# The softmax of two attentions, taken by pairs of heads instead of head by head

## The chip, the cores and the metric

The kernel runs as one program on one core of a Trainium2 chip. Its time is the device time of one execution in microseconds (us); the runs of a kernel are compared by their median. Five engines work beside each other, each with its own list of instructions in fixed order: TensorE (PE; its weight loads are PEld), VectorE (DVE), ScalarE (ACT), GpSimd (POOL) and SyncE (SP, which only issues transfers here). An engine waits where its list has a wait on a semaphore that another engine counts up.

## The reference

Two blocks of a network work on 256 tokens of width 1024, all in fp32. The first has a recurrent layer and then an attention with 16 heads over a window of 128 tokens; the second has a gated feed-forward network, a mixer of two attentions with 8 heads each, and a second feed-forward network. Two of the three attentions have a softmax. The first has a sink, a learned number per head that takes part in the maximum and the sum but has no value:

```python
    s = jnp.where(valid[None, :, None, None], s + alibi[None, None], -jnp.inf)
    sink = sinks.astype(jnp.float32).reshape(N_KV_HEADS, GROUP)[None, None, :, :, None, None]
    m = jnp.maximum(jnp.max(s, axis=-1, keepdims=True), sink)
    p = jnp.exp(s - m)
    denom = jnp.sum(p, axis=-1, keepdims=True) + jnp.exp(sink - m)
    p = (p / denom).astype(v.dtype)
    o = jnp.einsum('bnkgqs,bnskd->bnqkgd', p, vb)
```

The second (MoBA, 8 heads) is, at this length, a causal softmax attention over all 256 tokens without sinks. Everything else is matrix products with weights that are read once from memory (134 MB).

## The kernel before

Most of the kernel is products with weights. A weight matrix comes in halves of a chunk (128x1024 numbers). SP loads a half into `stage`, ACT rounds it to `w_hi` (helper `hi`, L933), DVE subtracts to get the rest `w_lo` (helper `lo`, L1373), and PE multiplies hi by hi, hi by lo and lo by hi (L480, L488). `w_hi` and `w_lo` are rings of four halves: half n can be made once PE is done with half n-4.

The two softmax attentions stand in the middle of such products. Each is a software pipeline over rounds r, one head to a round, and every engine has its own loop over r. The 128 queries of each of the two token blocks lie on the partitions; a head's scores are 128x384 numbers, block 0 with 128 keys and block 1 with 256, so each head has two maxima, two sums and two exponentials.

- PE, even r: `scores_of_two` (L719) makes the scores of heads r and r+1 in banks 0 and 1; it first waits until both maxima of the two heads before have been taken, since these still read the same two banks. Then, each r from LAG = 4 on, `turn(r-4)` (L731) transposes the normalised probabilities of head r-4 into bank 2 or 3; `turn(n)` waits for head n's normalisation, and for the copy that empties its bank from head n-2 (`t_out` at least n-1). In odd r, from 7 on, `values_of_two` (L738, L741) multiplies with v. At the rounds in `SWA_FILL` a half of a product (24 matmuls) is put in between, in the second attention one half in each round. From r = 17 on the first attention's output product begins (`gated_out`).
- DVE, each r: `masked_max(r)` (L1677) adds the bias or mask, writes the scores to one of five buffers in SBUF, and takes the maxima; the negated maxima `ntop` (L1680) release ACT. `inverse_sum(r-2)` adds the sink's exponential (L1689) and inverts (L1692). Then come the other pieces of `SWA_LO`: a `w_lo`, or copies out of banks.
- ACT, each r: `softmax_exp(r)` takes two exponentials with the negated maximum as bias and the sum as second output, and in the first attention a third, of the sink. Then `turned(r-4)` copies head r-4's transposed probabilities out of bank 2 or 3; only then follows the `w_hi` of `SWA_HI`, if any. After round 15 ACT loads the table for silu, which the gates of the output product need.
- POOL, each r: makes the distance bias of head r+3 (L460) and normalises head r-2 in two instructions (L448, L450).

Heads of the first attention are 0 to 15 below, those of the second are 16 to 23.

## Time and profile before

| | us |
|---|---|
| median of 3 runs (838.83 to 838.92) | 838.84 |
| the profiled execution, whole | 838.82 |
| its span in the trace | 837.0 |
| PE busy / DVE busy / ACT busy / POOL busy | 806.7 / 551.7 / 468.7 / 124.9 |
| first attention, 189 to 230 us: PE busy of 41.0 | 35.22 |
| second attention, 485 to 522 us: PE busy of 37.0 | 37.00 |

Busy times are sums over an engine's instructions, overlaps counted once. The 1.8 us between span and whole are start and end of the program, which no engine's instructions fill. PE is busy for 96% of the span, so only its idle time (30.3 us in all), and what would make it longer, can move the end. In a timeline row the bracket gives the engine's idle time before the instruction and who ended it.

### The profile page before, as it was taken

What the parts mean: (1) busy time and instruction counts of PE and PEld (TensorE: products, weight loads), DVE (VectorE), ACT (ScalarE), POOL (GpSimd) and SP (SyncE); (2) the same over time, 40 slices, a digit from 0 to 9 for tenths busy, and PEclk for the clock granted to TensorE, in tenths of its full rate; (3) what the DMA queues carried; (4) which work ended last, traced back from release to release, by engine and by line L of the source; (5) the groups of instructions that cost most, each with busy time, mean ns of one, the idle gap of its engine ahead of it and who ended that gap; (6) DMA issues with size and microseconds to landing.
All of it is one profiled execution on the core that took longest, in us unless ns stands there. A gap on an engine that the chain in (4) does not pass through costs nothing.

```text
span 837.0 us, 16462 instructions
## 1 busy us (share of the span) xinstructions
PE 806.7 (96%) x6371; PEld 775.1 (93%) x6371; DVE 551.7 (66%) x811; ACT 468.7 (56%) x732; POOL 124.9 (15%) x143
## 2 busy tenths in 40 slices
PE   5999799999899999999999999999999999999997
PEld 5999799897699999999999999998999999999885
DVE  6987995867658766666448755455577766666443
ACT  5679844767856544454345455655747454444433
POOL 9315620215503000000003003000001200000000
PEclk9999899999999999999999999999999999999999
DMA  8624347462236666655655544443545666665651
GB/s 257 211 76 130 122 152 228 128 192 89 95 95 208 202 184 189 180 177 181 193 176 154 179 147 143 134 126 122 179 134 183 192 200 189 186 176 179 181 193 50
DMA packets 104104, 136.35 MB, mean 163 GB/s; under 512 B 5049, under 2 KB 92529, under 8 KB 104049
## 3 DMA queue, kind: packets, MB, share of 16 engines
q1 hardware_dynamic: 102288, 133.26, 51.9%
q0 software_dynamic: 1600, 2.28, 1.0%
q8 instruction: 39, 0.64, 0.3%
q14 instruction: 17, 0.13, 0.1%
q10 hardware_dynamic: 160, 0.05, 0.0%
HBM read 134.51 MB, written 1.05 MB: 162 GB/s over the span
## 4 chain that ended last, share of the span: by engine, by line
PE 74%; ACT 4%; DVE 4%; POOL 3%; issue 1%; POOLq 0%; ACTq 0%; DVEq 0%
PE bank L480 54%; PE bank L540 7%; PE bank L488 7%; POOL arena L432 2%; ACT a_hi L933 2%; DVE w_lo L1373 1%; PE bank L719 1%; ACT w_hi L933 1%; ACT arena L933 1%; PE bank L738 1%; PE bank L731 1%; PE bank L896 1%; DVE arena L1677 1%; PE bank L884 1%; DVE a_lo L1408 0%
## 5 line engine op out<-in xcount | busy, mean ns | idle before, releaser
L480 PE MATMUL bank<-a_hi,w_hi 128*128 128x256 f32 (+1 forms) x1672 | 477.8, 286 | 11.1 <-DVE w_lo L1373 6.2
L480 PE MATMUL bank<-a_lo,w_hi 128*128 128x256 f32 (+1 forms) x1672 | 473.9, 283 | 0.0
L480 PE MATMUL bank<-a_hi,w_lo 128*128 128x256 f32 (+1 forms) x1672 | 473.7, 283 | 0.0
L1373 DVE TENSOR_TENSOR w_lo<-stage,w_hi 128x1024 fp32r<-128x1024 f32 x250 | 317.8, 1280 | 223.0 <-ACT w_hi L933 222.8
L933 ACT ACTIVATE w_hi<-stage 128x1024 fp32r<-128x1024 f32 x250 | 260.6, 1052 | 160.6 <-PE bank L480 115.0
L480 PEld LDWEIGHTS bank<-a_hi,w_hi 128*128 128x128 f32 x1672 | 321.5, 192 | 15.5 <-issue 7.9
L480 PEld LDWEIGHTS bank<-a_lo,w_hi 128*128 128x128 f32 x1672 | 321.7, 192 | 0.0
L480 PEld LDWEIGHTS bank<-a_hi,w_lo 128*128 128x128 f32 x1672 | 321.6, 192 | 0.0
L933 ACT ACTIVATE arena<-arena 128x512 f32<-128x512 f32 (+4 forms) x63 | 37.8, 605 | 76.1 <-DVE arena L1440 42.9
L432 POOL TENSOR_TENSOR arena<-arena 128x512 f32<-128x512 f32 x12 | 23.0, 1925 | 375.1 <-ACT arena L933 374.8
L488 PE MATMUL bank<-w_hi,a_hi 128*128 128x256 f32 x208 | 60.5, 291 | 1.7 <-DVE a_lo L1408 1.7
L488 PE MATMUL bank<-w_hi,a_lo 128*128 128x256 f32 x208 | 58.8, 283 | 0.0
L488 PE MATMUL bank<-w_lo,a_hi 128*128 128x256 f32 x208 | 58.8, 283 | 0.0
L933 ACT ACTIVATE a_hi<-arena 128x512 fp32r<-128x512 f32 (+3 forms) x49 | 29.6, 605 | 50.7 <-DVE arena L1784 15.0
L488 PEld LDWEIGHTS bank<-w_hi,a_hi 128*128 128x128 f32 x208 | 39.8, 191 | 2.9 <-DVE a_lo L1408 1.2
L488 PEld LDWEIGHTS bank<-w_hi,a_lo 128*128 128x128 f32 x208 | 39.9, 192 | 0.0
L488 PEld LDWEIGHTS bank<-w_lo,a_hi 128*128 128x128 f32 x208 | 39.8, 192 | 0.0
L540 PE MATMUL bank<-w_hi,a_lo 128*128 128x512 f32 x88 | 34.3, 390 | 0.0
L540 PE MATMUL bank<-w_hi,a_hi 128*128 128x512 f32 x88 | 34.2, 389 | 0.0
L540 PE MATMUL bank<-w_lo,a_hi 128*128 128x512 f32 x88 | 34.2, 389 | 0.0
L933 ACT ACTIVATE arena<-bank 128x384 f32<-128x384 f32 (+1 forms) x35 | 17.9, 513 | 26.9 <-PE bank L854 7.9
L933 ACT ACTIVATE arena<-arena,ntop 128x128 f32<-128x128 f32 (+1 forms) x48 | 21.4, 446 | 19.9 <-DVE ntop L1680 19.7
(178 smaller groups left out, 670.2 us busy)
## 6 DMA issues: line engine op xcount, KB each, us to landing
stage<-ffn_w_gate SPq DMA_DIRECT2D x44, 512.0 KB, 3.8
stage<-ffn_w_up SPq DMA_DIRECT2D x44, 512.0 KB, 3.8
stage<-ffn_w_down SPq DMA_DIRECT2D x44, 512.0 KB, 3.6
stage<-w_in SPq DMA_DIRECT2D x40, 512.0 KB, 3.5
stage<-a_w_in SPq DMA_DIRECT2D x24, 512.0 KB, 4.8
stage<-b_w_in SPq DMA_DIRECT2D x16, 512.0 KB, 4.0
stage<-a_w_out SPq DMA_DIRECT2D x12, 512.0 KB, 3.8
stage<-b_w_out SPq DMA_DIRECT2D x8, 512.0 KB, 3.6
```

What stands on the lines that cost most here:

```text
L432: pool.tensor_tensor(tiles(SQ + a, w), tiles(SQ + a, w), tiles(SQ + b, w), ALU.add).then_inc(sq_add, 1)
L480: mm = pe.matmul(dst, w[:, slot, c:c + P], a[:, k, :] if isinstance(k, int) else wide(a[:, bass.ds(k, 1), :]), start=start and n == 0, sto ...
L488: mm = pe.matmul(dst, a[:, k, tb * P:(tb + 1) * P], w[:, slot, c:c + n], start=start and i == 0, stop=stop and i == 2, skip_group_check=True)
L540: mm = pe.matmul(token_bank(tb, h)[:, :], a[:, k, t], w[:, slot, c], start=False, stop=w is w_hi and a is a_hi, skip_group_check=True)
L719: mm = pe.matmul(bank[i][:, c:c + w], q[r, t * T + c:t * T + c + P], k[r, 0:keys], start=True, stop=True)
L731: mm = pe.transpose(bank[2 + n % 2][:, c * P:(c + 1) * P], p[:, c * P:(c + 1) * P], ident)
L738: pe.matmul(bank[o][i * HD:(i + 1) * HD, c:c + T], v[i][0], w[i][:, 0:T], start=True, stop=False, skip_group_check=True)
L884: pe.matmul(z[:, 0:T], k[s, 0:P], q[s, 0:T], start=True, stop=True)
L896: pe.matmul(sums[:, 0:SC], con[:, TRI:TRI + P], sp_n, start=True, stop=False, skip_group_check=True)
L933: return nc.scalar.activation(out_, in_, func, **kw)
L1373: dve.tensor_tensor(w_lo[:, n % RING, 0:w], src, w_hi[:, n % RING, 0:w].bitcast(F32), ALU.subtract)\
L1677: dve.tensor_tensor_reduce(s[:, c:c + w], ps[:, c:c + w], bias[:, T - w:T], 1.0, floor, ALU.add, ALU.max, accum_out=top[:, 2 * n + q:2 * n ...
```

## The change

Both softmaxes are done by pairs of heads. On DVE, in even rounds only, `masked_max` runs for heads r and r+1 one behind the other, one instruction then negates all four maxima (`negated`), for the first attention another forms sink minus maximum for both heads, and `inverse_sums` adds and inverts for both heads of the pair before. On ACT, `softmax_of_two` takes the four exponentials of the pair in even rounds, and one of 128x4 for the two sinks, on an input that needs no bias; `turned(r-4)` stays one to a round behind it. POOL's normalisations wait for the pair's inverse. The score buffers go from five to six. PE's list of instructions and its waits are unchanged. The diff:

```diff
--- before.py
+++ after.py
@@ -86,6 +86,7 @@
 SWA_HI = {1: 11, 2: 12, 4: 13, 6: 14, 11: 15, 12: 16}
 SWA_LO = {2: 11, 3: 12, 7: 13, 10: 14, 12: 15, 15: 16}
 LAG = 4
+SCORE_BUFS = 6
 MIX_TURN = {5: 0, 6: 1, 7: 2, 8: 3}
 
 MOBA_FILL = [1] * 12
...
@@ -251,11 +252,11 @@
 
         def score_buf(n):
 
-            return flat[:, 24 * T + n % (LAG + 1) * SC:24 * T + (n % (LAG + 1) + 1) * SC]
+            return flat[:, 24 * T + n % SCORE_BUFS * SC:24 * T + (n % SCORE_BUFS + 1) * SC]
 
         def prob_t(n):
 
-            at = 24 * T + (LAG + 1 + n % 3) * SC
+            at = 24 * T + (SCORE_BUFS + n % 3) * SC
             return flat[:, at:at + SC]
 
         def dist_bias(n):
@@ -443,7 +444,7 @@
             square_sums(1)
             def normalise(n):
 
-                pool.wait_ge(den_inv, n + 1)
+                pool.wait_ge(den_inv, n // 2 + 1)
                 s = score_buf(n)
                 pool.tensor_scalar(s[:, 0:P], s[:, 0:P], rden[:, 2 * n:2 * n + 1], 1.0, ALU.mult, ALU.mult)\
                     .then_inc(p_norm, 1)
@@ -1147,15 +1148,17 @@
                 swa_slot(j)
             act.preload_act_table(ACT.Exp)
 
-            def softmax_exp(n, sinks=None):
-
-                act.wait_ge(s_neg, n + 1)
-                s = score_buf(n)
-                e = f(s[:, 0:P], s[:, 0:P], ACT.Exp, bias=ntop[:, 2 * n:2 * n + 1], accum_out=rsum[:, 2 * n:2 * n + 1])
-                e = f(s[:, P:SC], s[:, P:SC], ACT.Exp, bias=ntop[:, 2 * n + 1:2 * n + 2],
-                      accum_out=rsum[:, 2 * n + 1:2 * n + 2])
-                if sinks is not None:
-                    e = f(esink[:, 2 * n:2 * n + 2], ntop[:, 2 * n:2 * n + 2], ACT.Exp, bias=sinks)
+            def softmax_of_two(n, sinks):
+
+                act.wait_ge(s_neg, n // 2 + 1)
+                for i in (n, n + 1):
+                    s = score_buf(i)
+                    f(s[:, 0:P], s[:, 0:P], ACT.Exp, bias=ntop[:, 2 * i:2 * i + 1], accum_out=rsum[:, 2 * i:2 * i + 1])
+                    e = f(s[:, P:SC], s[:, P:SC], ACT.Exp, bias=ntop[:, 2 * i + 1:2 * i + 2],
+                          accum_out=rsum[:, 2 * i + 1:2 * i + 2])
+                if sinks:
+                    act.wait_ge(s_sink, n // 2 + 1)
+                    e = f(esink[:, 2 * n:2 * n + 4], esink[:, 2 * n:2 * n + 4], ACT.Exp)
                 e.then_inc(p_exp, 1)
 
             def turned(n):
@@ -1175,8 +1178,8 @@
                 f(tiles(8 + 2 * c, 2), tiles(8 + 2 * c, 2), ACT.Silu).then_inc(silu_b, 1)
 
             for r in range(NQ + LAG):
-                if r < NQ:
-                    softmax_exp(r, sink[:, r:r + 1])
+                if r < NQ and r % 2 == 0:
+                    softmax_of_two(r, True)
                 if r == NQ:
                     gate_silu(0)
                 if r >= LAG:
@@ -1281,8 +1284,8 @@
                 mix_slot(j)
             act.preload_act_table(ACT.Exp)
             for r in range(NH + 5):
-                if r < NH:
-                    softmax_exp(NQ + r)
+                if r < NH and r % 2 == 0:
+                    softmax_of_two(NQ + r, False)
                 if LAG <= r < NH + LAG:
                     turned(NQ + r - LAG)
                 if r >= 1:
@@ -1670,24 +1673,31 @@
             def masked_max(n, bias, floor):
 
                 dve.wait_ge(s_done, n + 1)
-                if n > LAG:
-                    dve.wait_ge(t_done, n - LAG)
+                if n >= SCORE_BUFS:
+                    dve.wait_ge(t_done, n - SCORE_BUFS + 1)
                 s, ps = score_buf(n), bank[n % 2]
                 for q, (c, w) in enumerate(((0, P), (P, T))):
                     dve.tensor_tensor_reduce(s[:, c:c + w], ps[:, c:c + w], bias[:, T - w:T], 1.0, floor, ALU.add, ALU.max,
                                              accum_out=top[:, 2 * n + q:2 * n + q + 1]).then_inc(s_max, 1)
-                dve.wait_ge(s_max, 2 * n + 2)
-                dve.tensor_scalar(ntop[:, 2 * n:2 * n + 2], top[:, 2 * n:2 * n + 2], -1.0, 1.0, ALU.mult, ALU.mult)\
-                    .then_inc(s_neg, 1)
-
-            def inverse_sum(n, sinks):
-
-                dve.wait_ge(p_exp, n + 1)
-                c = slice(2 * n, 2 * n + 2)
+
+            def negated(n, sinks):
+
+                dve.wait_ge(s_max, 2 * n + 4)
+                c = slice(2 * n, 2 * n + 4)
+                dve.tensor_scalar(ntop[:, c], top[:, c], -1.0, 1.0, ALU.mult, ALU.mult).then_inc(s_neg, 1)
+                if sinks:
+                    two = lambda t: t[:, c].rearrange("p (h b) -> p h b", h=2)
+                    by = sink[:, n:n + 2].unsqueeze(2).to_broadcast([P, 2, TB])
+                    dve.tensor_tensor(two(esink), by, two(top), ALU.subtract).then_inc(s_sink, 1)
+
+            def inverse_sums(n, sinks):
+
+                dve.wait_ge(p_exp, n // 2 + 1)
+                c = slice(2 * n, 2 * n + 4)
                 total = rsum
                 if sinks:
                     dve.tensor_tensor(esink[:, c], esink[:, c], rsum[:, c], ALU.add).then_inc(den_sum, 1)
-                    dve.wait_ge(den_sum, n + 1)
+                    dve.wait_ge(den_sum, n // 2 + 1)
                     total = esink
                 dve.reciprocal(rden[:, c], total[:, c]).then_inc(den_inv, 1)
 
@@ -1711,11 +1721,14 @@
                 dve.tensor_copy(tiles(16 + 2 * b, 2), bank[6 + b % 2][:, :]).then_inc(o_out, 1)
 
             for r in range(NQ + 2):
-                if r < NQ:
-                    dve.wait_ge(bias_ready, r + 1)
-                    masked_max(r, dist_bias(r), sink[:, r:r + 1])
-                if r >= 2:
-                    inverse_sum(r - 2, True)
+                if r % 2 == 0:
+                    if r < NQ:
+                        for n in (r, r + 1):
+                            dve.wait_ge(bias_ready, n + 1)
+                            masked_max(n, dist_bias(n), sink[:, n:n + 1])
+                        negated(r, True)
+                    if r >= 2:
+                        inverse_sums(r - 2, True)
                 if r in SWA_LO:
                     swa_slot(SWA_LO[r])
                 if r in (11, 14):
@@ -1873,10 +1886,13 @@
             for j in range(12):
                 mix_slot(j)
             for r in range(NH + 5):
-                if r < NH:
-                    masked_max(NQ + r, con[:, CMASK:CMASK + T], -3e38)
-                if 2 <= r < NH + 2:
-                    inverse_sum(NQ + r - 2, False)
+                if r % 2 == 0:
+                    if r < NH:
+                        for n in (NQ + r, NQ + r + 1):
+                            masked_max(n, con[:, CMASK:CMASK + T], -3e38)
+                        negated(NQ + r, False)
+                    if 2 <= r < NH + 2:
+                        inverse_sums(NQ + r - 2, False)
                 if r >= 1:
                     for j in fill(MOBA_FILL, 12, r - 1):
                         mix_slot(j)
```

Two places show what moves. The first is the end of the first attention on ACT (`arena,rsum<-arena,ntop` is an exponential with its sum, `esink` the sinks', `arena<-bank 128x384` the copy of a transposed head, `turned`). Before, rounds 14 and 15:

```order
L933 ACTIVATE arena,rsum<-arena,ntop 128x128 [waits s_neg]
L933 ACTIVATE arena,rsum<-arena,ntop 128x256
L933 ACTIVATE esink<-ntop,sink 128x2
L933 ACTIVATE arena<-bank 128x384 [waits o_done,t_done]
L933 ACTIVATE arena,rsum<-arena,ntop 128x128 [waits s_neg]
L933 ACTIVATE arena,rsum<-arena,ntop 128x256
L933 ACTIVATE esink<-ntop,sink 128x2
L933 ACTIVATE arena<-bank 128x384 [waits o_done,t_done]
L1187 ACT_TABLE_LOAD
```

After, the same two rounds:

```order
L934 ACTIVATE arena,rsum<-arena,ntop 128x128 [waits s_neg]
L934 ACTIVATE arena,rsum<-arena,ntop 128x256
L934 ACTIVATE arena,rsum<-arena,ntop 128x128
L934 ACTIVATE arena,rsum<-arena,ntop 128x256
L934 ACTIVATE esink<-esink 128x4 [waits s_sink]
L934 ACTIVATE arena<-bank 128x384 [waits o_done,t_done] x2
L1190 ACT_TABLE_LOAD
```

The copy of head 10, first `arena<-bank` row of either list, now stands behind the exponentials of both heads 14 and 15 instead of head 14's alone; the copy of head 11 follows it at once.

The second place is DVE in rounds 10 and 11 of the first attention (`arena,top<-bank,arena,sink` takes a maximum, each with an `ISA top` that reads it out). Before:

```order
L1677 ISA arena,top<-bank,arena,sink 128x128 [waits t_done,s_done,bias_ready]
L1677 ISA top 128x1
L1677 ISA arena,top<-bank,arena,sink 128x256
L1677 ISA top 128x1
L1680 TENSOR_SCALAR ntop<-top 128x2 [waits s_max]
L1689 TENSOR_TENSOR esink<-esink,rsum 128x2 [waits p_exp]
L1692 RECIPROCAL rden<-esink 128x2 [waits den_sum]
L1373 TENSOR_TENSOR w_lo<-stage,w_hi 128x1024 [waits hi_done]
L1677 ISA arena,top<-bank,arena,sink 128x128 [waits t_done,s_done,bias_ready]
L1677 ISA top 128x1
L1677 ISA arena,top<-bank,arena,sink 128x256
L1677 ISA top 128x1
```

After, from behind head 10's first maximum:

```order
L1680 ISA top 128x1
L1680 ISA arena,top<-bank,arena,sink 128x256
L1680 ISA top 128x1
L1680 ISA arena,top<-bank,arena,sink 128x128 [waits t_done,s_done,bias_ready]
L1680 ISA top 128x1
L1680 ISA arena,top<-bank,arena,sink 128x256
L1680 ISA top 128x1
L1687 TENSOR_SCALAR ntop<-top 128x4 [waits s_max]
L1691 TENSOR_TENSOR esink<-sink,top 128x4
L1699 TENSOR_TENSOR esink<-esink,rsum 128x4 [waits p_exp]
L1702 RECIPROCAL rden<-esink 128x4 [waits den_sum]
L1376 TENSOR_TENSOR w_lo<-stage,w_hi 128x1024 [waits hi_done]
```

Head 11's maxima stood behind head 10's negation, an inversion and a `w_lo`; now they follow head 10's directly, and the negation, the inversion and the `w_lo` come after them.

## Rows read from the trace of the kernel before

**Rows 1.** Windows: stretch, length, busy us (x instructions) per engine, clock, DMA, GB/s

```profile
189.00:230.00 41.00, 35.22 (x296) 28.94 (x295) 29.59 (x127) 33.34 (x107) 22.68 (x42) 1.00 0.28 91
230.00:267.00 37.00, 37.00 (x310) 35.99 (x308) 26.98 (x32) 21.56 (x31) 6.91 (x4) 1.00 0.44 132
485.00:522.00 37.00, 37.00 (x310) 34.19 (x309) 21.10 (x62) 21.75 (x51) 8.40 (x16) 1.00 0.42 130
```

**Rows 2.** PE timeline: start us, us, instruction, [idle before, releaser]; its waits

```profile
190.80 0.93 PE L719 MATMUL bank<-arena 64*128 64x128 f32 x8 [1.36 <-DVE top L1677]
...
205.30 0.93 PE L719 MATMUL bank<-arena 64*128 64x128 f32 x8 [0.25 <-DVE top L1677]
...
214.87 0.93 PE L719 MATMUL bank<-arena 64*128 64x128 f32 x8 [1.70 <-DVE top L1677]
...
223.95 0.52 PE L731 MATMUL bank<-con,arena 128*128 128x128 f32 x3 [0.75 <-ACT arena L933]
...
229.71 0.36 PE L480 MATMUL bank<-a_hi,w_hi 128*128 128x256 f32 x1 [1.24 <-issue]
```

**Rows 3.** PE timeline, scores (L719) and transposes (L731) that waited for nothing

```profile
202.12 0.93 PE L719 MATMUL bank<-arena 64*128 64x128 f32 x8
...
206.16 0.55 PE L731 MATMUL bank<-con,arena 128*128 128x128 f32 x3
...
210.65 0.93 PE L719 MATMUL bank<-arena 64*128 64x128 f32 x8
...
215.73 0.55 PE L731 MATMUL bank<-con,arena 128*128 128x128 f32 x3
...
220.20 0.93 PE L719 MATMUL bank<-arena 64*128 64x128 f32 x8
```

**Rows 4.** DVE timeline, two heads' maxima, and one w_lo piece

```profile
203.18 0.35 DVE L1677 CUSTOM_DVE_ANT_0 arena<-bank,arena,sink 128x128 f32<-128x128 f32 x1 [2.08 <-PE bank L719]
...
203.86 0.08 DVE L1677 DVE_READ_ACCUMULATOR2_ANT top<- 128x1 f32 x1
203.98 0.17 DVE L1680 TENSOR_SCALAR ntop<-top 128x2 f32<-128x2 f32 x1
...
204.39 0.35 DVE L1677 CUSTOM_DVE_ANT_0 arena<-bank,arena,sink 128x128 f32<-128x128 f32 x1
...
212.85 1.21 DVE L1373 TENSOR_TENSOR w_lo<-stage,w_hi 128x1024 fp32r<-128x1024 f32 x1
```

**Rows 5.** ACT timeline, last heads of the first attention

```profile
222.26 0.40 ACT L933 ACTIVATE arena<-arena,ntop 128x128 f32<-128x128 f32 x1 [0.53 <-DVE ntop L1680]
...
223.15 0.28 ACT L933 ACTIVATE esink<-ntop,sink 128x2 f32<-128x2 f32 x1
223.34 0.47 ACT L933 ACTIVATE arena<-bank 128x384 f32<-128x384 f32 x1
...
225.55 1.28 ACT L1187 ACT_TABLE_LOAD   x1
```

**Rows 6.** POOL timeline, a normalisation beside a w_lo piece

```profile
213.03 1.26 POOL L448 TENSOR_SCALAR arena<-arena,rden 128x128 f32<-128x128 f32 x1 [2.03 <-DVE rden L1692]
```

**Rows 7.** ACT groups by shape, 530 to 600 us: busy us, mean ns

```profile
L933 ACT ACTIVATE arena<-arena 128x384 f32<-128x384 f32 x24 | 12.5, 522 | 26.1 <-DVE arena L1892 19.8 <-DVE arena L1904 6.0
L933 ACT ACTIVATE arena<-arena,ones 128x384 f32<-128x384 f32 x8 | 4.9, 616 | 0.3
```

**Rows 8.** PE timeline, scores (L719) of the second attention

```profile
491.92 0.93 PE L719 MATMUL bank<-arena 64*128 64x128 f32 x8
...
498.72 0.93 PE L719 MATMUL bank<-arena 64*128 64x128 f32 x8
```

**Rows 9.** PE timeline, end of its longest idle stretch

```profile
101.07 0.58 PE L480 MATMUL bank<-a_hi,w_hi 128*128 128x256 f32 x1 [4.86 <-DVE w_lo L1373]
```

**Rows 10.** Windows in and behind that stretch

```profile
98.00:99.00 1.00, 0.00 (x0) 0.00 (x0) 1.00 (x1) 0.99 (x3) 0.77 (x1) 0.82 0.00 0
101.00:106.00 5.00, 4.93 (x25) 4.93 (x26) 5.00 (x6) 1.95 (x3) 2.07 (x2) 0.55 0.57 151
```

4 lines of the change are left out of this document (2 added, 2 removed).

## The prediction

> **What bounds the kernel now.** First the windows [rows 1]: in the second attention PE is busy 37.00 of 37.00 us, in the first 35.22 of 41.00, and then 37.00 of 37.00 again up to 267 us. So the second attention has no PE time to give. The first has 41.00 - 35.22 = 5.78 us of idle PE, and since PE is full behind it, whatever the first attention gains or loses by 229.7 us goes through to the end.
>
> Next PE's timeline in the first attention, for what ends its waits [rows 2]. Three scores wait for the maxima of the pair before (1.36 at 190.80, 0.25 at 205.30, 1.70 at 214.87); the transpose of head 12 at 223.95 waits 0.75 for a copy by ACT (`turned(10)`, which empties its bank); the output product at 229.71 waits 1.24. This makes 5.30 of the 5.78; two waits of under 0.3 are the rest. The transposes of head 4 at 206.16 and head 8 at 215.73 wait for nothing yet [rows 3], though they have the same condition as head 12's.
>
> **What the change makes of DVE's part.** Now scores follow a chain on DVE: scores at 202.12, maxima of the first head from 203.18 (1.06 later), of the second from 204.39 (1.21 on), next scores at 205.30 (0.91 on) [rows 2 to 4], together 3.18 us. The 1.21 hold head 1's maxima, a negation, a sum and an inverse. Paired, the second head's maxima start when the first head's last read-out starts, 203.86 - 203.18 = 0.68 on; the chain is 1.06 + 0.68 + 0.91 = 2.65. A full stop of DVE between the two would make that 0.80 instead (203.98 - 203.18), so 0.68 to 0.80; I take 0.68, since the maxima of one head already follow each other so. In rounds 10 and 11 a `w_lo` of 1.21 (212.85) stands in that chain too [rows 4], and goes behind it.
>
> What is won on its own: at 190.80 only a negation goes out of the chain, with its gap 0.12 (203.86 to 203.98) plus most of its 0.17: -0.2. At 214.87 the scores could start 2.65 after those at 210.65, at 213.30 instead of 214.87, or -1.57.
>
> **What it makes of ACT's part.** `turned(n)` stood behind the exponentials of one head and now stands behind those of two. The transpose of head n+2 needs it. Before, the transpose at 223.95 came 3.75 after the scores of heads 14 and 15 at 220.20 [rows 2, 3]: maxima, negation, one head's exponentials with its sink, the copy. Added to that path are: the second head's maxima before the common negation, 0.68 [rows 4]; the second head's two exponentials, 223.15 - 222.26 = 0.89 [rows 5]; taken off is something of the sink's exponential, which has no pointer operand any more. Instructions of the same shape, 128x384, take 0.616 us with one and 0.522 without [rows 7], so -0.09 (between 0 and -0.19, its whole step from 223.15 to 223.34 [rows 5]). The new path from scores to transpose is 3.75 + 0.68 + 0.89 - 0.09 = 5.23 us. It applies three times, for heads 4, 8 and 12.
>
> Step by step, all from times of before:
> 1. Scores of heads 6, 7: 202.12 - 0.2 = 201.9.
> 2. Transpose of head 4: 201.9 + 5.23 = 207.13, before 206.16: +0.97. PE would be there about 206, so it waits for a full microsecond where it waited for nothing.
> 3. From there to the scores of heads 10, 11 PE has its own work, 210.65 - 206.16 = 4.49 [rows 3] with a half of a product in it: 211.62.
> 4. Scores of heads 12, 13: 211.62 + 2.65 = 214.27, so -0.60. The large wait of 1.70 is gone; PE now waits some 0.2.
> 5. Transpose of head 8: 211.62 + 5.23 = 216.85, before 215.73: +1.12. What step 4 won is waited away at once, since this transpose hangs on the scores of heads 10, 11 and not on those of 12, 13.
> 6. Scores of heads 14, 15: 220.20 - 215.73 = 4.47 later [rows 3], 221.32.
> 7. Transpose of head 12: 221.32 + 5.23 = 226.55, before 223.95: +2.60.
> 8. The output product. On PE there are 229.71 - 1.24 - 223.95 = 4.52 us of work up to it [rows 2]: 226.55 + 4.52 = 231.07. On ACT: `turned(10)` starts 0.61 before the transpose (223.34 to 223.95), `turned(11)` follows at once, two copies of 0.47 at most, and then the table load, which comes 229.71 - 225.55 = 4.16 before the product [rows 2, 5]: 226.55 - 0.61 + 0.94 + 4.16 = 231.04. Both agree: 231.07, or +1.36. The old wait of 1.24 before this product takes up the rest of the +2.60.
>
> From 231 on PE is full as before, so the end moves by +1.36.
>
> **The other parts of the edit.**
> - Sinks minus maxima is one more small instruction on DVE a pair, and two negations, sums and inverses become one each. DVE is busy 29.6 of 41 us [rows 1]; off the chains above this costs or gives nothing. The subtraction runs beside the exponentials on ACT, about 1.8 us before it is used.
> - The sixth score buffer takes away the need to wait for a transpose issued later than the scores; without it the second maxima of a pair would wait for a transpose that stands behind their own scores on PE. It costs nothing.
> - Normalisations wait for the pair's inverse, and in round 10 a `w_lo` follows that inverse directly. Head 8's scaling beside that `w_lo` takes 1.26 us [rows 6]. The inverse is through about 1.06 + 0.68 + 0.80 + 0.5 = 3.04 after the scores; POOL starts 0.2 later, and with 1.26 for the first instruction and 0.5 for the second (estimate, the `w_lo` being over) head 8 is ready at 5.0, hidden behind 5.23 by 0.2. If the second were as slow, it would be +0.5. Keep that for the range.
> - Second attention: `turned` comes 5.2 after the scores here too, but the next scores come 498.72 - 491.92 = 6.80 later [rows 8] by PE's own work, and the transpose behind those. It is hidden by over 1.5 us. `w_hi` and `w_lo` are made up to three halves ahead there, and ACT and DVE are busy 21.8 and 21.1 of 37 us [rows 1], so their pieces may slip by the 1 to 2 us of a pair. I cost it at 0, and no gain is possible below 37.00 of 37.00.
>
> **The sum.** The profiled execution took 838.82 us (span 837.0), the median is 838.84, so a shift on the one is a shift on the other. 838.82 + 1.36 = 840.18, I say 840.2. The bounds: 0.80 for 0.68 in the three paths, +0.36; the sink's exponential as long as before, +0.27; POOL's second instruction, +0.3 beyond the cover; in the other direction the sink's step gone wholly, -0.3, and a shorter copy-to-transpose handover, -0.3. So this case spans 839.5 to 841.2.
>
> **Rivals.**
> A. ACT's copies are not late, and only DVE's part counts. For it: the waits in which the page of before shows most PE time all name DVE's maxima (1.36, 0.25, 1.70), and ACT has 7.7 idle us in this stretch (33.34 busy of 41.00) [rows 1, 2]. Against it: ACT's order puts the copy behind the second head, and 223.95 shows a transpose already waiting on just that copy. It would give -0.2 - 0.25 at the scores of heads 8, 9, then 210.20 + 2.65 = 212.85 for those of 12, 13, which is -2.0, and no loss after: 836.8 us.
> The Trainium skill, VectorE: DVE Perf Modes, section Rules for kernel authors, advises for chained operations to minimise the number of operations, not of semaphores. By it this edit should help, as ACT alone loses eight sink exponentials of 0.19 each, 1.5 us, giving 837.3. That would come true only where the engine is the bound throughout, and rows 2 show that here it is bound by what stands in front of what.
> B. The clock falls in the new wait. Before the transpose of head 12 PE is out of work about 3.0 after the scores (223.95 - 0.75 - 220.20 = 3.00), and waits 2.2 until 5.23. The granted clock has been full in all of this stretch [rows 1]. But when PE stopped at 101.07 - 4.86 = 96.21 [rows 9], the clock fell to its lower level (1.2 GHz) within the slice 98 to 99 (mean 0.82), and was at 0.55 on average over 101 to 106 with PE working again [rows 10], which lost 5 x 0.45 = 2.2 us. That stop was 4.86 us long, the one here would be 2.2, between two shorter ones. If the clock falls here too: 838.82 + 1.36 + 2.2 = 842.4, slower. It decides only if the level is lowered during the wait; if not, it costs nothing.
> The Trainium skill, TensorE: Matmul & The Clock Gate, section HAM oscillation, says that waits recurring between groups of matmuls make the clock fall again and again; this stretch would have four waits of 1 to 2 us instead of two, and full clock in the rows of before shows only that two were not enough.
> C. Gain and loss cancel: `turned` is late only for head 12, where its wait was seen before, as PE is behind by more than I work out at heads 4 and 8. Then the scores of heads 14, 15 come 0.6 earlier, the transpose of head 12 is 3.75 + 1.48 behind them at 224.83, and the output product follows at 224.83 + 4.52 = 229.35, -0.4: 838.5 us.
>
> **Chances.** My case 0.65, A 0.10, B 0.15, C 0.10. A difference of 0.2%, 1.7 us, is about what can be told from no change here. My case lies below that for the most part, say 0.44 of its 0.65 within and 0.21 above; A is faster, B slower, C within except for 0.01. So faster 0.11, same 0.53, slower 0.36. Range: my case's own is 839.5 to 841.2; to hold 8 in 10 it takes in C and part of B, 838.0 to 842.6.
>
> **What would show it.** Right: the transpose of head 4, four heads after its softmax, starts over 5 us after the scores of heads 6, 7, with a wait of about 1 us that ACT ends; likewise heads 8 (1.8) and 12 (over 2). Scores of heads 12, 13 wait under 0.5 instead of 1.70. PE is idle 7.1 us instead of 5.8 up to the output product, and the second attention stays without idle time. Wrong: transposes that wait for POOL or not at all; scores that still wait for DVE by more than 0.5; a granted clock under 1.00 around 225 to 230 us (that would be B); PE idle time in the second attention, where I have none.

## The result, and the profile after

The changed kernel takes 841.50 us (median of 8 runs, 839.98 to 842.74), the kernel before 838.88 us on the same chip (8 runs, 838.70 to 839.46). The ratio is 1.0031, 95% interval 1.0021 to 1.0040: slower by 2.6 us. The forecast was 840.2. Six of the eight times lie between 841.2 and 841.7, one at 840.0 and one at 842.7, and the gap of some 1.5 us below the six turns out to be a part of the answer.

The profiled execution took 841.37 us (span 839.5). Its page shows that the edit did make VectorE and ScalarE do less: 811 and 732 instructions became 787 and 724, busy time 551.7 and 468.7 us became these.

```profile
PE 809.3 (96%) x6371; PEld 777.8 (93%) x6371; DVE 548.1 (65%) x787; ACT 466.3 (56%) x724; POOL 122.1 (15%) x143
```

The windows, in the columns of [rows 1]: the first attention, the stretch behind it, the second attention, and then short stretches late in the first attention.

```profile
189.00:230.00 41.00, 33.83 (x275) 28.24 (x273) 26.52 (x109) 29.96 (x97) 22.02 (x42) 0.96 0.31 91
230.00:267.00 37.00, 37.00 (x310) 35.59 (x310) 25.51 (x32) 21.50 (x33) 4.43 (x3) 1.00 0.38 115
485.00:522.00 37.00, 37.00 (x310) 34.18 (x310) 20.21 (x54) 21.60 (x52) 6.54 (x16) 1.00 0.48 146
226.50:226.60 0.10, 0.10 (x4) 0.10 (x2) 0.00 (x0) 0.08 (x2) 0.10 (x1) 1.00 0.00 0
226.60:226.70 0.10, 0.10 (x3) 0.10 (x2) 0.00 (x0) 0.10 (x1) 0.10 (x1) 0.52 0.00 0
227.00:228.00 1.00, 1.00 (x7) 1.00 (x7) 0.00 (x0) 0.99 (x2) 1.00 (x3) 0.50 0.86 160
...
230.00:231.00 1.00, 1.00 (x10) 1.00 (x10) 0.60 (x1) 0.00 (x0) 0.00 (x0) 0.99 0.00 0
```

The second attention and the stretch from 230 us have no idle PE time, as before. In the first, PE is idle for 41.00 - 33.83 = 7.17 us instead of 5.78, and from 226.6 to 230.0 us the granted clock is at its lower level (0.50, that is 1.2 GHz) where before it was full.

PE's timeline, the instructions that answer to [rows 2] and [rows 3] (line numbers are one higher in this kernel: L720 scores, L732 transposes, L481 products of weights):

```profile
201.79 0.93 PE L720 MATMUL bank<-arena 64*128 64x128 f32 x8
...
207.00 0.52 PE L732 MATMUL bank<-con,arena 128*128 128x128 f32 x3 [1.01 <-ACT arena L934]
...
211.44 0.93 PE L720 MATMUL bank<-arena 64*128 64x128 f32 x8
...
214.07 0.93 PE L720 MATMUL bank<-arena 64*128 64x128 f32 x8
...
216.64 0.52 PE L732 MATMUL bank<-con,arena 128*128 128x128 f32 x3 [1.64 <-ACT arena L934]
...
221.08 0.93 PE L720 MATMUL bank<-arena 64*128 64x128 f32 x8
...
226.29 0.59 PE L732 MATMUL bank<-con,arena 128*128 128x128 f32 x3 [2.68 <-ACT arena L934]
226.57 0.54 PE L481 MATMUL bank<-a_hi,w_hi 128*128 128x256 f32 x1
...
231.02 0.49 PE L732 MATMUL bank<-con,arena 128*128 128x128 f32 x3
...
232.24 0.39 PE L481 MATMUL bank<-a_hi,w_hi 128*128 128x256 f32 x1
```

The waits of 0.25 and 1.70 us for VectorE's maxima are gone. In their place stand waits of 1.01, 1.64 and 2.68 us for ScalarE at the transposes of heads 4, 8 and 12 (a fourth, at head 3's, grew from 0.21 to 0.61 us, just ahead of head 4's). The last row is the output product: 232.24 where it was 229.71 [rows 2], 2.53 us later, and that is the whole difference of the two executions (841.37 - 838.82 = 2.55). It comes in two pieces. The transpose of head 12 is 226.29 - 223.95 = 2.34 us late, of which the wait of 1.24 us ahead of the old output product takes up all of itself; that leaves 1.10. The other piece is the half product behind the transpose: the first two thirds of its matmuls, up to 229.9 us, follow each other at 0.21 us instead of 0.12, it takes 231.02 - 226.57 = 4.45 us instead of the 2.95 of the one from 216.91 to 219.86 in the same trace, and the output product comes 5.95 us behind the transpose of head 12 and not 4.52. That is 1.43 us, and the granted clock in the windows above explains it.

What VectorE and ScalarE's timelines show of the new pair: the second head's maxima start 0.68 us after the first's, and the sinks' exponential without pointer operand takes 0.19 us instead of 0.28 [rows 5].

```profile
212.49 0.35 DVE L1680 CUSTOM_DVE_ANT_0 arena<-bank,arena,sink 128x128 f32<-128x128 f32 x1 [3.90 <-PE bank L720]
...
213.17 0.35 DVE L1680 CUSTOM_DVE_ANT_0 arena<-bank,arena,sink 128x128 f32<-128x128 f32 x1
...
213.96 0.17 DVE L1687 TENSOR_SCALAR ntop<-top 128x4 f32<-128x4 f32 x1
...
214.30 0.18 DVE L1702 RECIPROCAL rden<-esink 128x4 f32<-128x4 f32 x1
...
224.04 0.66 DVE L1721 COPY arena<-bank 128x512 f32<-128x512 f32 x1
224.62 1.22 DVE L1376 TENSOR_TENSOR w_lo<-stage,w_hi 128x1024 fp32r<-128x1024 f32 x1
```

```profile
225.58 0.19 ACT L934 ACTIVATE esink<-esink 128x4 f32<-128x4 f32 x1
225.68 0.84 ACT L934 ACTIVATE arena<-bank 128x384 f32<-128x384 f32 x2
```

POOL's timeline, the normalisations of head 8 and head 12:

```profile
214.57 1.26 POOL L449 TENSOR_SCALAR arena<-arena,rden 128x128 f32<-128x128 f32 x1 [3.38 <-DVE rden L1702]
215.81 0.48 POOL L451 TENSOR_SCALAR arena<-arena,rden 128x256 f32<-128x256 f32 x1
...
224.22 0.37 POOL L449 TENSOR_SCALAR arena<-arena,rden 128x128 f32<-128x128 f32 x1 [3.15 <-DVE rden L1702]
224.57 1.53 POOL L451 TENSOR_SCALAR arena<-arena,rden 128x256 f32<-128x256 f32 x1
```

Head 12 is normalised at 226.10, its transpose starts at 226.29. The wait names ScalarE, whose copy came last, but POOL was only 0.2 us ahead of it. The `[3.15 <-DVE rden]` tells why POOL is that late: the inverse of a pair's sums stands on VectorE behind the maxima of the next pair (213.96, 214.30), so it comes with the scores of that pair.

### The profile page after: what moved, and what is told of

Its sections match the earlier page's. It is cut to its first block, busy times and chain, and to the rows that moved or that the text cites. A ratio compares the mean times of both kernels' runs of the same rounds, so it can differ in the third digit from the quotient of the medians.

```text
span 839.5 us, 16430 instructions
## 1 busy us (share of the span) xinstructions
PE 809.3 (96%) x6371; PEld 777.8 (93%) x6371; DVE 548.1 (65%) x787; ACT 466.3 (56%) x724; POOL 122.1 (15%) x143
## 3 DMA queue, kind: packets, MB, share of 16 engines
HBM read 134.51 MB, written 1.05 MB: 161 GB/s over the span
## 4 chain that ended last, share of the span: by engine, by line
PE 73%; ACT 5%; DVE 4%; POOL 3%; issue 2%; POOLq 0%; ACTq 0%; DVEq 0%
PE bank L481 54%; PE bank L541 7%; PE bank L489 7%; POOL arena L433 2%; ACT a_hi L934 2%; ACT arena L934 2%; DVE w_lo L1376 1%; ACT w_hi L934 1%; PE bank L720 1%; PE bank L739 1%; PE bank L732 1%; PE bank L897 1%; DVE arena L1680 1%; PE bank L885 1%; DVE a_lo L1411 0%
## 5 line engine op out<-in xcount | busy, mean ns | idle before, releaser
L481 PE MATMUL bank<-a_hi,w_hi 128*128 128x256 f32 (+1 forms) x1672 | 478.9, 286 | 8.5 <-DVE w_lo L1376 5.4
L481 PE MATMUL bank<-a_lo,w_hi 128*128 128x256 f32 (+1 forms) x1672 | 474.8, 284 | 0.0
L481 PE MATMUL bank<-a_hi,w_lo 128*128 128x256 f32 (+1 forms) x1672 | 474.8, 284 | 0.0
L481 PEld LDWEIGHTS bank<-a_hi,w_hi 128*128 128x128 f32 x1672 | 322.7, 193 | 13.0 <-DVE w_lo L1376 6.2
L481 PEld LDWEIGHTS bank<-a_lo,w_hi 128*128 128x128 f32 x1672 | 322.8, 193 | 0.0
L481 PEld LDWEIGHTS bank<-a_hi,w_lo 128*128 128x128 f32 x1672 | 322.6, 193 | 0.0
L1443 DVE TENSOR_TENSOR arena<-bank,spread 128x512 f32<-128x512 f32 x47 | 32.0, 684 | 1.4 <-PE bank L481 1.3
```

The lines of the kernel that those rows point to most:

```text
L481: mm = pe.matmul(dst, w[:, slot, c:c + P], a[:, k, :] if isinstance(k, int) else wide(a[:, bass.ds(k, 1), :]), start=start and n == 0, sto ...
L1443: return dve.tensor_tensor(y, x, by, ALU.mult)
```

## The experiments

The theory taken into them: (1) the paired exponentials put ScalarE's copy 5.2 us behind the scores, and PE waits for it three times, which costs some 1.1 us; (2) PE's clock falls at the longest of these waits, which costs some 1.5 us more. Rivals: POOL's normalisation, the second attention or the moved buffers are to blame. All kernels of a group shared the runs of the kernel before, whose median was 838.87, 838.86 and 838.81 us in the three groups.

### ScalarE head by head again

In both attentions the exponentials go one head to a round again, each behind the pair's negation, the sinks' with the second head. VectorE keeps its pairs. The cut shows the loop of the first attention:

```
-                if r < NQ and r % 2 == 0:
-                    softmax_of_two(r, True)
+                if r < NQ:
+                    softmax_of(r, True)
...
```

> Only ACT's half of the change is undone: DVE still takes four maxima and one negation a pair, but ACT again does the exponentials of one head, the copy of a transposed head, then the other head's. Theory 1 (the copies behind two heads' exponentials cost the time): the path from scores to the transpose three rounds on is 5.2 us less one head's exponentials, 4.2 to 4.3 us; head 4's transpose waits for almost nothing, head 8's and head 12's about 0.8 and 1.3 us, the clock stays full near 226 us, the output product starts near 228.9 (changed kernel 232.24, before 229.71), and the kernel takes 837.9 to 838.3 us. Rival (DVE's pairing or POOL's later release is what costs): it stays at 840.5 to 841.5, with the waits of 1.0, 1.6 and 2.7 us still there.

Measured: 840.97 us (11 runs), ratio 1.0022 [1.0013, 1.0031]. Three runs lie at 839.5 to 839.7, eight at 840.8 to 841.4. The expectation missed by over 2 us; the time is the rival's, and the waits are still there. PE's waits at heads 8 and 12 in the profiled execution, which was one of the three (839.51); head 4's, at 206.95, is like them:

```profile
216.32 0.55 PE L732 MATMUL bank<-con,arena 128*128 128x128 f32 x3 [1.34 <-POOL arena L451]
...
225.87 0.55 PE L732 MATMUL bank<-con,arena 128*128 128x128 f32 x3 [2.17 <-POOL arena L451]
```

The same three transposes start 0.05, 0.32 and 0.42 us earlier than after, and now name POOL. ScalarE's pair was late, but not alone.

### ScalarE's copy ahead of the pair's exponentials

```
+                if LAG <= r < NQ:
+                    turned(r - LAG)
                 if r < NQ and r % 2 == 0:
                     softmax_of_two(r, True)
                 if r == NQ:
                     gate_silu(0)
-                if r >= LAG:
+                if r >= NQ:
                     turned(r - LAG)
```

> All of the change stays, but in the first attention ACT's copy of round r goes ahead of the pair's four exponentials (the transposed head is there earlier than the maxima are). Theory 1: the transposes of heads 4, 8 and 12 no longer hang on the exponentials; what is next is the normalisation on POOL, about 4.3 us after the scores, 5.0 where a w_lo piece runs beside it (head 8). So waits of 0.1, 0.6 and 1.5 us instead of 1.01, 1.64 and 2.68, no fall of the clock there, output product near 229.3, kernel 838.2 to 838.7 us. Rival (ACT is simply too busy with a pair at a time, whatever the order): the waits only move, 840 us or more.

Measured: 840.95 us (11 runs, two at 839.7 and 839.8, nine at 840.7 to 841.1), ratio 1.0020 [1.0011, 1.0030]. Missed in the same way. The profiled execution is one of the nine (840.95). PE's wait at head 12, and the clock behind it:

```profile
225.88 0.64 PE L732 MATMUL bank<-con,arena 128*128 128x128 f32 x3 [2.54 <-POOL arena L451]
```

```profile
226.00:230.00 4.00, 4.00 (x22) 4.00 (x23) 1.50 (x3) 3.33 (x5) 2.24 (x6) 0.57 0.40 131
```

The same window in the experiment before, whose profiled execution was one of its three quick ones:

```profile
226.00:230.00 4.00, 4.00 (x34) 3.72 (x36) 1.42 (x4) 3.56 (x6) 2.21 (x6) 1.00 0.43 131
```

There the clock stayed full, behind a wait of 2.17 us: PE did 34 instructions in these 4 us, here 22. So of two kernels whose transposes come at the same times, the quick execution has the full clock and the slow one the fall.

Two quite different remedies on ScalarE leave the transposes at the same times (225.87, 225.88), so theory (1) lacked a part: POOL is late too, a few tenths of a microsecond less. Nor is it the rival's ScalarE that is too busy, since the waits now name POOL. Set beside the quick execution of the kernel after (839.98), the quick ones here, 839.5 to 839.8, show what either remedy buys: 0.2 to 0.5 us.

### Matmuls in the wait of head 12

Twenty matmuls whose result nobody reads, ahead of the transpose of head 12, into a bank that is free.

```
+                if r == NQ:
+                    pe.wait_ge(q_raw, 3)
+                    for i in range(20):
+                        pe.matmul(bank[5][:, 0:T], a_hi[:, 0, 0:P], a_hi[:, 0, :], start=True, stop=True,
+                                  skip_group_check=True)
```

> The changed kernel with 20 more matmuls of 128x256 on PE, whose result nobody reads, put in the wait of head 12's transpose (2.68 us idle): nothing waits less, PE is only not idle. Theory 2 (half of the loss is the clock, which falls in this wait and stays at its lower level until 229.9): the granted clock stays at 1.00 from 222 to 233 us, the half product behind it takes 2.96 us instead of 4.45, and the kernel takes 839.8 to 840.1 us, 1.5 below the changed kernel though it has more work. Rival (the clock's record tells nothing of the time, or it falls anyway as the waits before it remain): 841.3 or more, the same or longer by the 2.4 us added.

Measured: 841.51 us (8 runs; 839.90 and 840.18, the others 841.4 to 841.7), ratio 1.0026 [1.0016, 1.0037]. Missed for the median; the two quick runs lie about where it was expected. The windows of the profiled execution say what happened (at 216 and 220 us the mean clock is 0.93 and 0.86):

```profile
217.00:220.00 3.00, 3.00 (x16) 3.00 (x15) 2.93 (x10) 3.00 (x11) 2.61 (x5) 0.50 0.52 175
...
222.00:236.00 14.00, 13.90 (x119) 12.11 (x119) 7.54 (x21) 9.99 (x23) 4.28 (x8) 1.00 0.18 65
```

The clock holds where the wait was filled, and falls at 216.9 us, just behind the wait of 1.64 us at head 8, which was left as it was. Inconclusive as it stands: the price is the same, the place another.

### Matmuls in all three waits

The same with 6, 11 and 20 matmuls at heads 4, 8 and 12.

```
+                if r in (8, 12, NQ):
+                    b, q, count = {8: (4, 2, 6), 12: (4, 2, 11), NQ: (5, 3, 20)}[r]
+                    pe.wait_ge(q_raw, q)
+                    for i in range(count):
+                        pe.matmul(bank[b][:, 0:T], ...)
```

> The kernel after with matmuls that nobody reads in the waits of heads 4, 8 and 12 (6, 11 and 20 of them, 0.12 us each), so that TensorE is busy in all three. The order of everything else and the late copies stay. Theory that the clock falls in these waits and costs 1.5 us in most executions: 839.8 to 840.2 in all runs, clock full from 205 to 236 us. Rival 'the waits alone cost all of it': 841.2 to 841.7.

Measured: 840.01 us, ratio 1.0010 [1.0001, 1.0019], and all 11 runs between 839.91 and 840.21. A hit. PE's timeline at head 12 and behind it, and the window from head 8 on:

```profile
223.67 2.65 PE L763 MATMUL bank<-a_hi 128*128 128x256 f32 x20
226.43 0.52 PE L732 MATMUL bank<-con,arena 128*128 128x128 f32 x3
...
230.87 0.39 PE L481 MATMUL bank<-a_hi,w_hi 128*128 128x256 f32 x1
```

```profile
217.00:236.00 19.00, 18.89 (x161) 16.94 (x160) 12.20 (x33) 13.85 (x34) 8.14 (x15) 1.00 0.24 85
```

Head 12 is transposed no earlier than after (226.43 against 226.29), the copies are as late as ever, and yet the kernel is 841.50 - 840.01 = 1.49 us faster, because the 4.45 us half product runs at the full clock. So the 2.64 us of the change split into 840.01 - 838.86 = 1.15 for the waits and 1.49 for the clock. This fits the median of the first filler run too: there a fall came at an unfilled wait, in six of eight executions by their times.

### The inverse ahead of the next pair's maxima

VectorE inverts a pair's sums at the start of its round; nothing else moves.

```
                 if r % 2 == 0:
+                    if r >= 2:
+                        inverse_sums(r - 2, True)
                     if r < NQ:
                         for n in (r, r + 1):
                             ...
                         negated(r, True)
-                    if r >= 2:
-                        inverse_sums(r - 2, True)
```

> The kernel after with one thing moved: VectorE inverts a pair's sums ahead of the next pair's maxima, not behind them, so GpSimd can normalise heads 4, 8 and 12 about 3 us earlier and beside no split of a weight tile. ScalarE still reads the transposed head out behind the pair's exponentials. Theory 'two things arrive together, each within 0.2 us of the other': ScalarE's copy alone still sets the waits at heads 4, 8 and 12 (1.0, 1.6, 2.7 us, released by ScalarE), so the time stays at 841.0 to 841.6. Rival 'GpSimd is what is late and ScalarE only beside it': the waits shrink by more than half and the time is 838.5 to 839.5.

Measured: 841.71 us (8 runs, 840.76 to 843.11), ratio 1.0035 [1.0024, 1.0045]; the time is 0.1 us above the band expected for ScalarE alone, and 2 us from the rival's. Head 12 waits as after (and head 8, 1.64 us, too):

```profile
226.66 0.69 PE L732 MATMUL bank<-con,arena 128*128 128x128 f32 x3 [2.67 <-ACT arena L934]
```

Head 4 waited 0.52 instead of the 1.0 expected, since an earlier transpose had waited 0.80 already.

### The inverse and the copy first

Two edits together, each of which took one late thing away: ScalarE's copy ahead of the pair's exponentials, and the inverse ahead of the next pair's maxima.

> The same as the run with the inverse first, and ScalarE's copy of a round ahead of that round's exponentials as well. Each of the two alone leaves the other in place; the theory that both are late together says that the three waits go only here: waits under 0.3 us at heads 4, 8 and 12, the clock full from 211 to 236 us, and 837.6 to 838.6 us, 2.5 us or more under the kernel after. Rival 'the clock falls anyway, or a third thing is late (the maxima behind the inverse, which waits for the exponentials)': 839.5 or more.

Measured: 837.54 us (11 runs, 837.37 to 837.74), ratio 0.9982 [0.9973, 0.9991]. That is 0.06 us below the expected band, and 4.0 us under the kernel after. PE's waits, and POOL at head 8:

```profile
204.35 0.52 PE L732 MATMUL bank<-con,arena 128*128 128x128 f32 x3 [0.91 <-POOL arena L451]
...
214.43 0.55 PE L732 MATMUL bank<-con,arena 128*128 128x128 f32 x3
...
221.32 0.52 PE L732 MATMUL bank<-con,arena 128*128 128x128 f32 x3 [1.02 <-POOL arena L451]
...
228.57 0.36 PE L481 MATMUL bank<-a_hi,w_hi 128*128 128x256 f32 x1 [1.46 <-issue]
```

```profile
211.81 0.48 POOL L451 TENSOR_SCALAR arena<-arena,rden 128x256 f32<-128x256 f32 x1
```

Head 8 (214.43) waits for nothing, nor do heads 4 and 12. Head 8 is normalised at 212.3 instead of 216.3 and outside the shadow of a weight split. The granted clock is full throughout. What is left is 0.91 and 1.02 us for POOL at heads 3 and 11, the second of their pairs, which was not expected, and the wait ahead of the output product. Copy first alone gives 840.95, inverse first alone 841.71, neither 841.50: the 4 us come only with both, some 1.5 of them from the clock, which by the times fell in none of the 11 runs, and the rest from the waits. This is the pattern of two late things behind one wait.

### The half products ahead of the transposes

On PE, the half products of rounds 8, 12 and 16 run before their round's transpose and not behind it; VectorE, ScalarE and POOL are as after.

```
+                if r in (8, 12, 16):
+                    swa_half(SWA_FILL[r])
                 if LAG <= r < NQ + LAG:
                     turn(r - LAG)
                 ...
-                if r in SWA_FILL:
+                if r in SWA_FILL and r not in (8, 12, 16):
```

> The changed kernel, with the half products of rounds 8, 12 and 16 put on PE in front of the transpose of the round instead of behind it. ACT's order is untouched. Theory 1 (PE waits since it stands at the transpose too early, the copies being late): the half products, 2.96 us each, cover the waits of 1.01, 1.64 and 2.68; the scores of heads 14, 15 come near 218.6 instead of 221.08; then ACT's chain to the output product (9.7 us after these scores) is the bound, near 228.3, with PE idle some 2.6 us before it. The kernel takes 837.4 us if the clock stays up there and 838.9 if it falls. Rival (the ring of weights or the scores are the bound instead): the waits come back at the half products or the scores, 840 us or more.

Measured: 837.38 us (11 runs, 837.22 to 837.51), ratio 0.9981 [0.9971, 0.9990], on the expected number. PE's timeline:

```profile
216.96 0.82 PE L732 MATMUL bank<-con,arena 128*128 128x128 f32 x6
...
224.84 0.82 PE L732 MATMUL bank<-con,arena 128*128 128x128 f32 x6
```

The copies are still late, but 3 us of PE's own work stand in front of the instruction that needs them (heads 8 and 9 in the row at 216.96, heads 12 and 13 at 224.84). The three waits are gone, and the granted clock is full throughout. PE still waits 0.61 and 0.70 us for ScalarE at heads 3 and 11, and 1.67 ahead of the output product.

The same edit in the kernel before, without pairs:

> The kernel before (head by head) with the half products of rounds 8, 12 and 16 ahead of the transpose of their round on TensorE, as in the run of the kernel after with the product first. Theory that pairs are worth something once the late copies are covered: here the 1.70 us wait of the scores at 214.9 us stays, since it stands ahead of the product, and only the 0.75 at 223.95 us can go: 838.1 to 838.9, so that the pairs' order is worth 0.7 us or more at the product-first order. Rival 'all of the gain is the reordering': 837.2 to 837.6, as with pairs.

Measured: 838.92 us, ratio 1.0001 [0.9992, 1.0010], at the upper end of the band.

```profile
214.90 0.93 PE L719 MATMUL bank<-arena 64*128 64x128 f32 x8 [1.09 <-DVE top L1679]
```

In this order of PE the pairs are worth 838.92 - 837.38 = 1.5 us, and the order by itself is worth nothing: PE gets to the scores of heads 12 and 13 as late as before, at 214.90 (214.87 in [rows 2]), and the wait of 0.75 us that goes at head 12 comes back as 0.56 instead of 0.27 at head 11 and as 1.68 instead of 1.24 ahead of the output product.

### Pairs in the second attention alone

The first attention is head by head as before (its sinks' exponential with pointer too); the second is as after; six score buffers in both.

> Pairs in the second attention alone (its maxima, exponentials and inverses as in the kernel after); the first attention head by head as in the kernel before, both with six score buffers. The second attention has TensorE busy throughout in both kernels, so the theory says no change: 838.8 to 839.0. Rival 'part of the 2.6 us comes from the second attention or from the moved buffers': 839.4 or more.

Measured: 839.07 us, ratio 1.0002 [0.9993, 1.0011]. PE is busy throughout in the second attention:

```profile
485.00:522.00 37.00, 37.00 (x311) 34.31 (x310) 20.21 (x54) 21.58 (x51) 6.50 (x16) 1.00 0.47 143
```

The 0.07 us over the expected band are not resolved by the interval, nor are the 0.2 us over the kernel before. What can be resolved of the change's cost is in the first attention.

### Both remedies and the product first

> Pairs with the copy first, the inverse first and the half products ahead of the transposes. Each of the two remedies alone brought the time to 837.4 to 837.5, with the output product then late behind the chain of table load, Silu, product and split (1.46 and 1.67 us of wait ahead of it). If that chain is what bounds now, both remedies together bring little: 837.0 to 837.5. Rival 'the remaining waits of 0.9 and 1.0 us at heads 5 and 11 are what bounds': about 836.0 to 836.6.

Measured: 838.59 us (838.47 to 838.68), ratio 0.9997 [0.9988, 1.0006]. Missed both ways: two remedies of 4 us each make 2.9 together. ScalarE's, VectorE's and PE's timeline show the loop that closes:

```profile
209.87 0.49 ACT L936 ACTIVATE arena<-bank 128x384 f32<-128x384 f32 x1 [1.75 <-PE bank L732]
...
218.54 0.49 ACT L936 ACTIVATE arena<-bank 128x384 f32<-128x384 f32 x1 [0.99 <-PE bank L732]
```

```profile
212.24 0.16 DVE L1703 TENSOR_TENSOR esink<-esink,rsum 128x4 f32<-128x4 f32 x1 [3.30 <-ACT esink L936]
...
220.90 0.16 DVE L1703 TENSOR_TENSOR esink<-esink,rsum 128x4 f32<-128x4 f32 x1 [0.74 <-ACT esink L936]
```

```profile
214.17 0.93 PE L720 MATMUL bank<-arena 64*128 64x128 f32 x8
...
222.34 0.52 PE L732 MATMUL bank<-con,arena 128*128 128x128 f32 x3 [1.37 <-POOL arena L451]
...
229.56 0.35 PE L481 MATMUL bank<-a_hi,w_hi 128*128 128x256 f32 x1 [1.38 <-issue]
```

The loop closes twice. With the product first, head 4's transpose comes only at 209.35 (206.46 with the two remedies alone); with the copy first, ScalarE's exponentials of heads 8 and 9 stand behind the copy of that transpose (209.87); with the inverse first, VectorE's maxima of heads 10 and 11 stand behind the sums of those exponentials (212.24), so the scores of heads 12 and 13 come at 214.17 instead of 213.58. The second time round it is the transpose of head 8 (218.01), the exponentials of heads 12 and 13 (behind the copy at 218.54) and the sums and maxima from 220.90 on. The output product starts 229.56 - 228.57 = 0.99 us later than with the two remedies alone, as the time is (1.05); 0.59 of it stem from the first time round.

The expectation speaks of a wait at head 5 that remains; the row (204.35 above) is head 3's.

### The table of Silu a round earlier

This was put on that kernel and on the one with the product first alone, since the wait ahead of the output product names no engine and the chain in front of it runs over ScalarE's table load.

```
-                if r == NQ - 1:
+                if r == NQ - 2:
                     act.preload_act_table(ACT.Silu)
```

> As the run with both remedies, and ScalarE loads the table of Silu a round earlier, right behind the last pair's exponentials and ahead of the copy of head 11. By the chain (exponentials, table load 1.28, Silu 0.63, product 0.69, high part 0.62, low part 0.69, output product) that takes 0.4 us from the path to the output product: 0.3 to 0.5 us under the run with both remedies. If the chain does not bound, no difference, or slower by what head 11's late copy costs.

> The kernel after with the half products ahead of the transposes (837.4 before), and the table of Silu loaded right behind the last pair's exponentials, ahead of two copies of 0.47 us. Theory that the chain to the output product bounds: 0.6 to 0.85 us less, 836.5 to 836.8. Rival 'the copies are then late for heads 12 and 13': 837.2 or more.

Measured: 838.56 and 837.26 us (ratios 0.9997 [0.9988, 1.0006] and 0.9980 [0.9971, 0.9989]), that is 0.03 and 0.12 us under the kernels without. Both expectations missed. ScalarE's timeline in the second of them:

```profile
223.24 1.28 ACT L1186 ACT_TABLE_LOAD   x1
...
225.29 0.63 ACT L936 ACTIVATE arena<-arena 128x512 f32<-128x512 f32 x1
```

The first Silu starts at 225.29, with the load behind the copies it was 225.26. The load and the copies (224.53) only changed places: ScalarE has no idle time there, and all of them still stand ahead of the Silu. To put the copies behind the Silu might shorten the chain; it was not tried.

837.3 to 837.5 us is the best that was found, by either road, 1.3 to 1.6 us under the kernel before and 4 us under the kernel after.

## Why the prediction was right, and where it was not

The forecast of 840.2 was 1.3 us short of the 841.50 measured. Its range (838.0 to 842.6) holds that time, but its own case (839.5 to 841.2) does not: the range reaches there by the part taken in for rival B. By its own threshold of 1.7 us the outcome is slower, to which it gave 0.36, and not no change, to which it gave 0.53.

Right, by its steps: scores of heads 6 and 7 at 201.79 (forecast 201.9), transposes of heads 4, 8 and 12 at 207.00, 216.64 and 226.29 (207.13, 216.85, 226.55), scores of heads 10 and 11, 12 and 13, 14 and 15 at 211.44, 214.07 and 221.08 (211.62, 214.27, 221.32). The path from scores to transpose was 5.20 to 5.21 us (5.23), from the terms 0.68 and -0.09 that the trace after shows as such. PE was idle for 7.17 us up to the output product (7.1). The second attention cost nothing that can be resolved (839.07 against 838.86). What was won at heads 12 and 13 (scores at 214.07 instead of 214.87) was waited away at the next transpose, as step 5 had it. Executions in which the clock stayed full are where the forecast put them: 839.98 for the kernel after, 840.01 with the waits filled.

The step that failed is step 8, the output product at 231.07. The 4.52 us of PE work behind the transpose of head 12 were taken from the trace of before, at the full clock. In the profiled execution they took 5.95 us, 3.4 of them at the lower one. The waits alone came to +1.15 us by the run with all three filled (forecast +1.36); the clock came to +1.49, a term that the likeliest case had at zero. It was in the text as rival B with a chance of 0.15 and a price of 2.2 us. The mechanism came, in the profiled execution and by their times in seven of the eight, at a smaller price: only 3.4 us of work ran slowly here, not 5. The waits were known to be longer than before, and [rows 9, 10] had shown the clock falling in a stop of PE; a chance of 0.15 was too low for what came in seven of eight. Rival B also says that a fall costs nothing unless it comes during the wait. It came behind it: PE was at work again from 226.29, the clock fell at 226.60, and the half product paid for it.

The page of the Trainium skill that was named there, TensorE: Matmul & The Clock Gate, section HAM oscillation, has waits that recur between groups of matmuls lower the clock again and again. The trace agrees in part: the clock fell once in a profiled execution, at 226.6 us after and at 216.9 us in the first filler run, behind waits of 2.68 and 1.64 us that are shorter than those of the page's own example, and behind a wait of 2.17 us in the first experiment it did not fall. The prediction's "four waits of 1 to 2 us instead of two" is miscounted: [rows 2] have three over 1 us.

The sentence on POOL was right by its sum and wrong in what it made of it. It has head 8 "hidden by 0.2"; the trace shows 0.35 us there (216.29 against 216.64), and 0.2 at head 12 (226.10 against 226.29), which the sentence does not name. The slow instruction was the first of head 8, as worked out, and the second of head 12, since VectorE's copy came between the inverse and the weight split there. For the time this made no difference. For the remedy it made all of it: with ScalarE mended alone, the transposes moved by 0.05 to 0.42 us. The prediction treated the second latest arrival as cover and not as the next bound, and the first two expectations inherited that.

Of the rivals, A (836.8) and C (838.5) failed at the transposes of heads 4 and 8, which did wait. The rule named with A (the Trainium skill, VectorE: DVE Perf Modes, section Rules for kernel authors: minimise the number of operations) is a rule for VectorE's own time, and for that the trace agrees: VectorE was busy 3.6 us less, and ScalarE, to which the prediction extends it, 2.4. For the kernel's time it is not borne out, which is 2.6 us more. Where nothing is queued behind the wrong thing, the pairs do pay: 1.5 us with the product first.

## What to carry to other kernels

Batching two steps of a pipeline delays the first one's consumers by the second one's work; follow every queue in which something unrelated stands behind the batch, and for each wait that appears write down the two latest arrivals, not only the last, since mending one buys just the gap between them. When a change lengthens TensorE's waits by microseconds, price the work behind the wait at the lower clock as well as at the full one. The only edit that cured the late inputs by itself here was to put independent work ahead of the instruction that needs it, and cures must be tried together, since two that are good alone can close a loop.

## What the runs showed of the hardware

- TensorE's clock fell to its lower level (0.50, 1.2 GHz) behind waits of 1.64 (first filler run), 2.54 (copy first), 2.67 (inverse first) and 2.68 us (after), with short bursts of work ahead of them, 0.1 to 0.3 us after TensorE was at work again, and was full again 3 to 4 us later. It did not fall behind a wait of 2.17 us in the first experiment's profiled execution (839.51 us), nor behind the 1.64 us of the kernel after. The times of one kernel group about 1.5 us apart (three and eight runs in the first experiment). The kernel before has ten of the 93 runs that the three groups shared at 840.3 to 840.6 too, and one run of the kernel after and two with the inverse first lie at 842.7 to 843.1; none of these was profiled, so that they are falls too, or two falls, is not shown. With the three waits filled by matmuls nobody reads, all 11 times lie within 0.3 us.
- A GpSimd instruction that overlaps VectorE's split of a weight tile takes as long as the split lasts: 1.26 instead of 0.37 us for 128x128, 1.53 instead of 0.48 for 128x256, beside 1.2 us of `w_lo`. Beside VectorE's copy out of PSUM (224.04) it took its usual 0.37. By the Trainium skill, GPSIMD Engine Reference, section Specifications, the two share SBUF interfaces and contend with VectorE instructions that have two SBUF inputs; the trace agrees, and `w_lo` is such a one.
- A ScalarE activation of 128x4 without pointer operand took 0.19 us, one of 128x2 with one 0.28 [rows 5].
